# A hybrid decoder layer: first weight piece in two halves with a PSUM bank per column block, first norm by token half, 17 products of ones ahead of the first transposes

## What is computed

```
h = x
h = h + ssd_mixer(rms_norm(h, mixer_norm), w_in, conv_w, ..., w_out)
h = h + cross_attention(rms_norm(h, xattn_norm), rms_norm(mem, mem_norm), xa_w_q, xa_w_kv, xa_w_o)
h = h + moe_ffn(rms_norm(h, ffn_norm), w_router, w_gate_up (32 x 1024 x 2048), w_down (32 x 1024 x 1024))
out = rms_norm(h, final_norm)

ssd_mixer:  proj = h @ w_in                      # 1024 x 5152: z 2048, xbc 3072, dt 32
            xbc  = silu(causal_conv4(xbc) + conv_b)
            dt   = softplus(proj_dt + dt_bias)   # then a chunked scan over 2 chunks of 128 tokens
```

## Time and profile before

| | |
|---|---|
| median of 3 runs | 1261.46 us (1261.38 to 1263.63) |
| the profiled execution's own time | 1264.04 us |
| its span | 1262.2 us |
| mean granted PE clock | 0.994 of 2.4 GHz |
| PE busy | 1173.2 us (93%) |
| DVE, ACT busy | 390.8 us, 265.4 us |
| DMA | 454.28 MB, mean 360 GB/s |

### The profile page before, as it was taken

How to read it: one execution, slowest core, us unless ns; L and a number is a source line. 1 busy time by engine, 2 the same in 40 slices (tenths; PEclk the granted TensorE clock), 3 DMA queues, 4 the chain that set the end, 5 groups by cost and what they waited for, 6 DMA issues and landing times.

```text
span 1262.2 us, 15351 instructions
## 1 busy us (share of the span) xinstructions
PE 1173.2 (93%) x6172; PEld 617.9 (49%) x6172; DVE 390.8 (31%) x705; ACT 265.4 (21%) x409; POOL 7.5 (1%) x27
## 2 busy tenths in 40 slices
PE   7999999999999999999889899999999998999996
PEld 6998887888733433333333333334433333333432
DVE  5887676645411211111111111212111111122112
ACT  6555444445210101010100001101101011011102
POOL 1000000000000000000000000000000000000000
PEclk9999999999999999999999999989999999999999
DMA  9454323478799999999999999999999999999996
GB/s 323 166 200 135 133 71 131 152 309 302 286 414 427 428 429 428 429 428 429 427 428 430 428 429 427 429 427 428 427 429 429 427 428 429 387 427 430 426 426 255
DMA packets 55654, 454.28 MB, mean 360 GB/s; under 512 B 6396, under 2 KB 6564, under 8 KB 30532
## 3 DMA queue, kind: packets, MB, share of 16 engines
q1 hardware_dynamic: 55440, 453.74, 87.0%
q10 hardware_dynamic: 180, 0.07, 0.0%
HBM read 452.74 MB, written 1.05 MB: 360 GB/s over the span
## 4 chain that ended last, share of the span: by engine, by line
PE 52%; DMA 42%; DVE 3%; SPq 1%; issue 1%; ACT 1%; DVEq 1%; ACTq 0%
DMA ring<-in_moe_w_down 41%; PE ps L882 13%; PE ps L906 11%; PE ps L559 3%; PE ps L561 3%; PE ps L560 3%; PE ps L916 2%; PE ps L858 2%; PE ps L574 2%; PE ps L576 2%; PE ps L575 2%; PE ps L693 1%; DMA wring<-in_ssd_w_in 1%; DVE wlo L1397 1%; PE ps L893 1%; SPq L430 1%
## 5 line engine op out<-in xcount | busy, mean ns | idle before, releaser
L906 PE MATMUL ps<-ring,wring 128*64 128x512 f32 x960 | 216.8, 597 | 54.7 <-DMA ring<-in_moe_w_down 54.7
L882 PE MATMUL ps<-ring,wring 128*64 128x512 f32 x1024 | 223.3, 594 | 0.0
L906 PEld LDWEIGHTS ps<-ring,wring 128*64 128x64 f32 x960 | 64.9, 137 | 194.8 <-issue 110.8
L1026 ACT ACTIVATE wring<-ps 128x512 f32<-128x512 f32 (+2 forms) x101 | 52.4, 534 | 501.6 <-PE ps L882 431.0
L1725 DVE COPY wring<-ps 128x512 f32<-128x512 f32 x32 | 22.1, 691 | 405.1 <-PE ps L882 405.1
L882 PEld LDWEIGHTS ps<-ring,wring 128*64 128x64 f32 x1024 | 72.1, 137 | 139.7 <-issue 139.6
L1733 DVE TENSOR_TENSOR wring<-ps,bguT 128x512 f32<-128x512 f32 x64 | 41.2, 686 | 302.6 <-PE ps L893 302.6
L882 PE MATMUL ps<-mid,wring 128*64 128x512 f32 x512 | 114.6, 600 | 1.0 <-DVE wring L1733 1.0
L1026 ACT ACTIVATE ysb<-ps 128x512 f32<-128x512 f32 x36 | 21.5, 598 | 272.1 <-PE ps L906 252.3
L882 PEld LDWEIGHTS ps<-mid,wring 128*64 128x64 f32 x512 | 35.8, 138 | 68.6 <-issue 68.3
L858 PEld LDWEIGHTS ps<-wring 128*128 128x128 f32 x480 | 55.8, 192 | 23.5 <-issue 23.5
(11 more groups left out here) (316 smaller groups left out, 1407.1 us busy)
## 6 DMA issues: line engine op xcount, KB each, us to landing
ring<-in_moe_w_gate_up SPq DMA_DIRECT2D x64, 2048.0 KB, 23.1
ring<-in_moe_w_down SPq DMA_DIRECT2D x60, 2048.0 KB, 25.5
mid<-in_moe_w_gate_up SPq DMA_DIRECT2D x32, 2048.0 KB, 23.4
wring<-in_moe_w_gate_up SPq DMA_DIRECT2D x16, 2048.0 KB, 26.4
hs<-in_moe_w_gate_up SPq DMA_DIRECT2D x16, 2048.0 KB, 27.9
wring<-in_ssd_w_in SPq DMA_DIRECT2D x10, 2048.0 KB, 8.2
wring<-in_xa_w_kv SPq DMA_DIRECT2D x4, 2048.0 KB, 8.2
wring<-in_ssd_w_out SPq DMA_DIRECT2D x4, 2048.0 KB, 7.8
```

Source lines behind the costliest of these rows:

```text
L882: last = mm(ps[a][SLOTS * half:SLOTS * (half + 1), :], xs[:, m, c % 2, :], w[:, kk, c0:c0 + 512], start=s + kk == 0, stop=s + kk == GP)
L906: last = mm(ps[D_BANK][SLOTS * half:SLOTS * (half + 1), :], act[:, k, :], w[:, kk, 512 * half:512 * (half + 1)], start=k == 0, stop=k == K ...
L1026: return nc.scalar.activation(out_, in_, func, **kw)
```

## The change

1. x's two token halves get a semaphore each (`ld_x[t]`), and ACT starts on half 0 when it has landed; ACT waits for the first POOL step alone instead of all constants.
2. Piece 0 is loaded by two transfers, row blocks 0 to 3 (`w_first`) and 4 to 7 (`w_ready[0]`). `first_projection` replaces `project_T`: all four column blocks with row blocks 0 to 3, then all four with 4 to 7, each block summed in a bank of its own (0, 1, 6, 7). `u_ps` is raised after blocks 0 and 1, and after 2 and 3, of the second pass.
3. PE makes 17 products `ones` x `ones` (128 x 128 float32) into bank 0 as soon as `ones` is there; nothing reads them.
4. The transposes of the parameter rows go behind the transposes of token half 0. On DVE the copy to `parT` goes behind both halves of the norm, and the constants `iota0`, `sel`, ... behind the copies of `xT`.
5. DVE copies row blocks 0, 1, 4, 5 of `xT`, ACT 2, 3, 6, 7. dt's products use bank 4 instead of 6. Convolutions of piece 0 read the new banks.

The diff, cut to its core:

```diff
+        def u_out(p, b, m):
+
+            return ps[(0, 1, 6, 7)[2 * b + m]][:, 0:SEQ] if p == 0 else ps[2 * (p % 2) + b][:, SEQ * m:SEQ * (m + 1)]
...
-                sp.dma_start(h[:, t, :], x[P * t:P * (t + 1), :]).then_inc(ld_x, 16)
+                sp.dma_start(h[:, t, :], x[P * t:P * (t + 1), :]).then_inc(ld_x[t], 16)
             for r0, v in ((16, mem_norm), (24, ssd_norm), (40, ffn_norm)):
                 n = v.shape[0] // P
                 sp.dma_start(rows_b[r0:r0 + n, :], v.rearrange("(c p) -> c p", p=P)).then_inc(ld_rows, 16)
-            sp.dma_start(wpiece(0), pieces[0]).then_inc(w_ready[0], 16)
+            sp.dma_start(wpiece(0)[:, 0:4, :], pieces[0][:, 0:4, :]).then_inc(w_first, 16)
+            sp.dma_start(wpiece(0)[:, 4:8, :], pieces[0][:, 4:8, :]).then_inc(w_ready[0], 16)
...
-            pe.wait_ge(cst_done, 1)
-            pe.wait_ge(ld_rows, 112)
-            tr(ps[7][:, 0:120], rows_a[0:120, :], ident[0:120, 0:120])
-            tr(ps[7][:, 128:176], rows_b[0:48, :], ident[0:48, 0:48]).then_inc(par_ps, 1)
+            pe.wait_ge(cst_step, 1)
+            for _ in range(WARM):
+                mm(ps[0][:, 0:P], ones, ones, start=True, stop=True)
+            pe.wait_ge(cst_step, 2)
+
+            def parameters(t):
+                pe.wait_ge(ld_rows, 112)
+                tr(ps[7][:, 0:120], rows_a[0:120, :], ident[0:120, 0:120])
+                tr(ps[7][:, 128:176], rows_b[0:48, :], ident[0:48, 0:48]).then_inc(par_ps, 1)
...
-            norm_transposes(0, xn0, 2)
+            norm_transposes(0, xn0, 2, parameters)
...
-                        last = mm(ps[6][HEADS * j:HEADS * (j + 1), 0:SEQ], wdt[:, 4 * half + j, :],
+                        last = mm(ps[4][HEADS * j:HEADS * (j + 1), 0:SEQ], wdt[:, 4 * half + j, :],
...
-            def project_T(n, banks, src, done, guard):
-
-                w = take(n)
-                for b in range(2):
-                    guard(b)
-                    for m in range(2):
-                        for n_, k in enumerate((0, 4, 1, 5, 2, 6, 3, 7)):
-                            if b == m == 0:
-                                pe.wait_ge((nt_dve, nt_act)[k // 4], k % 4 + 1)
-                            c0 = (2 * b + m) * P
-                            last = mm(ps[banks[b]][:, SEQ * m:SEQ * (m + 1)], w[:, k, c0:c0 + P], src[:, k, :],
-                                      start=n_ == 0, stop=n_ == KD - 1)
-                    last.then_inc(done, 1)
+            def first_projection():
+
+                w = wpiece(0)
+                pe.wait_ge(par_sb, 1)
+                for half in range(2):
+                    pe.wait_ge(*((w_ready[0], 16) if half else (w_first, 16)))
+                    for b in range(2):
+                        for m in range(2):
+                            for k in range(4 * half, 4 * half + 4):
+                                if b == m == 0:
+                                    pe.wait_ge((nt_dve, nt_act)[k // 2 % 2], 2 * half + k % 2 + 1)
+                                c0 = (2 * b + m) * P
+                                last = mm(u_out(0, b, m), w[:, k, c0:c0 + P], xT[:, k, :],
+                                          start=k == 0, stop=k == KD - 1)
+                        if half:
+                            last.then_inc(u_ps, 1)
...
-            project_T(W_U, (0, 1), xT, u_ps, lambda b: None)
+            first_projection()
...
+                    if n == 0:
+                        act_.wait_ge(ld_x[t], 16)
...
-            def norm_out(n, dst, gains, bank0=0):
...
+            def first_rows():
+
+                for k in (2, 3, 6, 7):
+                    act_.wait_ge(nt_ps, k // 2 + 1)
+                    fn(xT[:, k, :], ps[2 + k // 2][:, SEQ * (k % 2):SEQ * (k % 2 + 1)], ACT.Copy,
+                       scale=parT[:, g_mix + k:g_mix + k + 1]).then_inc(nt_act, 1)
...
-            act_.wait_ge(cst_done, 1)
+            act_.wait_ge(cst_step, 1)
             load_sqrt()
-            act_.wait_ge(ld_x, 32)
             norm_stats(0, h, xn0)
             act_.wait_ge(par_sb, 1)
-            norm_out(0, xT, g_mix, 2)
+            first_rows()
...
+                    last = fn(cv[:, n % 4, m, :], u_out(p, b, m), ACT.Identity,
...
-            dve.wait_ge(cst_done, 1)
-            v.tensor_scalar(iota0[:, :], iota[:, 0:NE], -1.0, None, ALU.add)
-            dve.drain()
-            v.tensor_scalar(sel[:, :], iota0[:, :], col[:, 1:2], None, ALU.is_equal)
-            dve.drain()
-            v.memset(acx[64:128, :, :], 1.0)
-            v.memset(nacx[0:64, :, :], 1.0)
-            v.tensor_reduce(ingrp[:, :], sel[:, :].rearrange("p (g j) -> p g j", g=GROUPS), AX_X, ALU.add)
-            v.tensor_reduce(by8[:, :], sel[:, :].rearrange("p (g j) -> p j g", g=GROUPS), AX_X, ALU.add)
-            dve.wait_ge(par_ps, 1)
-            v.tensor_copy(parT[:, 0:120], ps[7][:, 0:120])
-            v.tensor_copy(parT[:, 120:168], ps[7][:, 128:176]).then_inc(par_sb, 1)
...
-            def norm_out(n, dst, gains, bank0=0):
...
+            def first_rows():
+
+                for k in (0, 1, 4, 5):
+                    dve.wait_ge(nt_ps, k // 2 + 1)
+                    v.tensor_scalar(xT[:, k, :], ps[2 + k // 2][:, SEQ * (k % 2):SEQ * (k % 2 + 1)],
+                                    parT[:, g_mix + k:g_mix + k + 1], None, ALU.mult).then_inc(nt_dve, 1)
...
-            for t in range(TC):
-                norm_chunk(0, t, xn0, h)
-            norm_out(0, xT, g_mix, 2)
+            norm_chunk(0, 0, xn0, h)
+            norm_chunk(0, 1, xn0, h)
+            dve.wait_ge(par_ps, 1)
+            v.tensor_copy(parT[:, 0:120], ps[7][:, 0:120])
+            v.tensor_copy(parT[:, 120:168], ps[7][:, 128:176]).then_inc(par_sb, 1)
+            dve.drain()
+            first_rows()
+            dve.wait_ge(cst_done, 1)
...
             dve.wait_ge(xz_hi, 1)
             v.tensor_tensor(xz[1], xT[:, :, :], xz[0].bitcast(F32), ALU.subtract)
             w_lo(1, 0)
...
+                        src = u_out(p, b, m)[:, 0:SEQ - back]
...
-            v.tensor_copy(dtT, ps[6][:, 0:SEQ]).then_inc(dtT_sb, 1)
+            v.tensor_copy(dtT, ps[4][:, 0:SEQ]).then_inc(dtT_sb, 1)
```

More of the change, by code:

```diff
@@ L59 @@
 HSLOTS = 4
+WARM = 17
 def build(nc, x, mem, mixer_norm, xattn_norm, mem_norm, ffn_norm, w_in, conv_w, conv_b, dt_bias, a_log,
@@ L211, in build @@
         sums = ps_all[:, 4 * 512:8 * 512].rearrange("p (t n c) -> p t n c", n=2, t=TC)
-        (ld_x, ld_mem, ld_rows, ld_small, ld_bg, ld_g, ld_bdn, ld_wdt, ld_wrt, cst_step, cst_done) = (
-            sem(n) for n in ("ld_x", "ld_mem", "ld_rows", "ld_small", "ld_bg", "ld_g", "ld_bdn", "ld_wdt",
+        ld_x = [sem(f"ld_x{t}") for t in range(TC)]
+        (ld_mem, ld_rows, ld_small, ld_bg, ld_g, ld_bdn, ld_wdt, ld_wrt, cst_step, cst_done) = (
+            sem(n) for n in ("ld_mem", "ld_rows", "ld_small", "ld_bg", "ld_g", "ld_bdn", "ld_wdt",
                              "ld_wrt", "cst_step", "cst_done"))
+        w_first = sem("w_first")
         w_ready = [sem(f"w_ready{s}") for s in range(3)]
@@ L532, in dt_tokens @@
                 for t in range(TC):
-                    last = mm(ps[6][:, SEQ + HEADS * t:SEQ + HEADS * (t + 1)], dtT[:, P * t:P * (t + 1)], sel[:, :],
+                    last = mm(ps[4][:, SEQ + HEADS * t:SEQ + HEADS * (t + 1)], dtT[:, P * t:P * (t + 1)], sel[:, :],
                               start=True, stop=True)
                 last.then_inc(dt_ps, 1)
-            def project_T(n, banks, src, done, guard):
-                w = take(n)
-                for b in range(2):
-                    guard(b)
-                    for m in range(2):
-                        for n_, k in enumerate((0, 4, 1, 5, 2, 6, 3, 7)):
-                            if b == m == 0:
-                                pe.wait_ge((nt_dve, nt_act)[k // 4], k % 4 + 1)
-                            c0 = (2 * b + m) * P
-                            last = mm(ps[banks[b]][:, SEQ * m:SEQ * (m + 1)], w[:, k, c0:c0 + P], src[:, k, :],
-                                      start=n_ == 0, stop=n_ == KD - 1)
-                    last.then_inc(done, 1)
+            def first_projection():
[13 more added lines that the diff above has]
+                            last.then_inc(u_ps, 1)
             def split_tokens(n, t, bank, x_hl, k0=0, ks=range(KD), start=True, stop=True):
@@ L1083, in tap @@
                     w = convw_c + 3 * NCONV + c0 + m
-                    last = fn(cv[:, n % 4, m, :], ps[2 * (p % 2) + b][:, SEQ * m:SEQ * (m + 1)], ACT.Identity,
+                    last = fn(cv[:, n % 4, m, :], u_out(p, b, m), ACT.Identity,
                               scale=parT[:, w:w + 1], bias=parT[:, convb_c + c0 + m:convb_c + c0 + m + 1])
@@ L1397, in w_lo @@
                 v.tensor_tensor(lo_, raw_, hi.bitcast(F32), ALU.subtract).then_inc(wl_ok, 1)
-            for t in range(TC):
-                norm_chunk(0, t, xn0, h)
-            norm_out(0, xT, g_mix, 2)
+            norm_chunk(0, 0, xn0, h)
```

(13 more changed lines are left out.)

## The result

Over 22 runs of each kernel, the changed one took 1264.88 us (median; 1263.09 to 1267.33) and the one before 1263.55 us (1261.38 to 1265.13). The ratio is 1.0014, with a 95% interval of 1.0008 to 1.0019: 1.0 to 2.4 us slower, within the 0.2% that the chances call "same". The two medians differ by 1.33 us, where +1.2 us was forecast; the time itself, 1264.88, lies above the stated range, which ended at 1263.9.

A forecast was written before the change was run, and what follows sets the result against it. DVE, fed by piece 1's landing, was taken to set the start of `dt_tokens`, and PE the pace after it. Nothing gained plus 1.2 us of slow clock on 1261.46 gave 1262.7 us, range 1260.8 to 1263.9.

The forecast's parts named there:

- the first term of the sum: The base for the whole kernel: median of earlier runs, 1261.46 us, to which 1.2 us were added.
- What bounds the kernel: Up to 36 us: piece 1's landing, ACT's rounding, then DVE until `dt_tokens` at 34.73; PE sets the pace afterwards.
- Start of the projection: First projection on PE: half 0 of x 1.1 us sooner, first transpose about 8.2, projection starting about 10.3.
- The 17 products: PE's start: they end between 5.2 and 9.0 and buy fast transposes, about 1 to 1.8 us off the path.
- Projection, banks, order: First projection keeps 14.05 us, ending about 24.3; `tap(0)` isn't delayed, and moved banks and constants cost nothing.
- even with a start at 12.7: First `u_ps` at 23.2 plus 1.00 for `tap(0)` would still come before `conv(0)` at 24.59.
- Transfers: SP's queue: piece 1 lands at 18.13 again despite one more issue; 0 us taken, bounds 0 and 4.7.
- The wait: PE before `dt_tokens` waits 2.9 us for DVE's copy (between 0.5 and 3.7), instead of 0.5.
- The clock: Behind PE's wait before `dt_tokens` the clock falls to half, costing 1.2 us of a full 1.45.
- The allowance for slow time inside the wait: At PE's wait before `dt_tokens`: 1.2 us taken instead of 1.45, since part of the slow stretch may lie there.
- says the same of such gaps: Claim that the Trainium skill, too, has a gap between bursts of products bring back TensorE's half-rate clock.
- the level and the scatter: Whole kernel: a base of 1261.46 us, with 0.7 us (range's low end) and 0.6 us (high end) of scatter.

The follow-up runs named there:

- e1: The changed kernel with 12 unread products of ones filling PE's wait before `dt_tokens`; ratio 0.9996 to the kernel before.
- e2: The changed kernel with `dt_tokens` moved behind the second pair of column blocks of piece 1; ratio 0.9984 to the kernel before.
- e6: The changed kernel with piece 0 loaded by one transfer again, both passes of the projection waiting for it; ratio 1.0009 to the kernel before.
- e8: The changed kernel with `dt_tokens` behind the second pair, DVE's second low half of piece 3 before `conv(3)`, and the 264 us wait filled; ratio 0.9977.
- e10: The changed kernel with `dt_tokens` behind the second pair, the 264 us wait filled, and piece 3 split earlier on ACT and DVE; ratio 0.9967, 1259.19 us.
- e5: The kernel before with only the 17 products of ones added ahead of the parameter transposes; ratio 0.9998 to the kernel before.
- e3: The changed kernel without the 17 products of ones at the start; ratio 0.9997 to the kernel before.
- e4: The kernel before with only `dt_tokens` moved behind the second pair of column blocks of piece 1; ratio 1.0012 to the kernel before.
- e11: The changed kernel with 5 unread products of ones in PE's wait before `dt_tokens`; ratio 0.9997 to the kernel before.
- e7: The kernel before with 9 products of ones in PE's wait at 264 us, ahead of the query products; ratio 0.9995.

## Why the prediction was right, and where it was wrong

The mechanism held: nothing gained on the path, a longer wait of PE, and the clock behind it. The step that failed is the first term of the sum, the level of 1261.46 us to which the 1.2 us were added; the runs put it at 1263.55.

**What bounds the kernel: right.** `dt_tokens` waits for DVE, DVE for piece 1; e1 and e2 show it from both sides.

**Start of the projection: right.** 9.98 against 10.3, with the first transpose at 7.46 against 8.2. ACT began on x 1.3 us sooner (4.77 against 6.09) and not 1.1; the rest is that the estimate left the two parameter copies before the first norm on DVE's way, which the change had moved. First half landed 6.2 us after its issue, at 9.0, against 9.5.

**The 17 products: right.** 5.41 us, between the bounds of 3.8 and 7.6, over before the transposes.

**Projection, banks, order: right.** 14.05 us again, end 23.96 against 24.3; `tap(0)` not delayed. That it would be covered "even with a start at 12.7" was reckoned at the fast clock alone; e6, with a start at 12.10 and a slow stretch behind it, kept DVE waiting 1.06 us. The constants that moved behind the norm cost nothing: DVE still stood idle 4.30 us before the first low half of piece 1.

**Transfers: right.** Piece 1 landed at 17.75, not later. The 0.4 us that it came sooner lies within the scatter: the kernels with the one transfer of before had ACT start on it between 17.69 and 18.16 in five profiles, those with the two halves between 17.68 and 17.78 in eight. A small help from the halves isn't excluded.

**The wait: right.** 2.88 us against 2.9.

**The clock: right in kind, a little too cheap.** I took 1.2 us from a full 1.45; the profile shows 1.51 and the ratio 1.0 to 2.4 us. The allowance for slow time inside the wait wasn't needed: the slow spacing began about 0.7 us after PE had resumed at 34.34. That the change in time came out so near is in part luck: in this profile the mark is 1.12 us late, the 1.51 less the 0.39 by which piece 1 happened to land sooner, and the sum took one fall in every run more than before, which no row then showed.
The Trainium skill's account ("TensorE: Matmul & The Clock Gate", Part 1, HAM oscillation) of a gap that brings the slow clock back is what the trace shows at 35 us. The gap of the page's example is longer than this wait of 2.88 us, so the prediction's "says the same of such gaps" claimed more than the page gives: that a wait of this length can be followed by a fall is what these runs show.

**Where it failed: the level and the scatter.** The sum was put on 1261.46, the median of three runs, and the range allowed 0.7 us of scatter. 22 runs gave 1263.55, and 89 runs beside the experiments spread from 1261.2 to 1265.6. Two of the three had fallen near the lower end; that was bad luck, but the spread was there to be seen: the third was 1263.63, and the text itself stated that the profiled execution took 1264.04, a quarter of the evidence then at hand, and took the level from the median all the same. It was an ordinary run. The 0.7 us is the distance of the profiled span, 1262.2, from that median; but a span is some 1.8 us shorter than its own execution's time (1264.04 here), so it compares unlike things. With a base of 1263.55 the sum gives 1264.75, 0.13 from the measured time, and the term that was mis-sized is the base, by 2.1 us.

**What the scatter is made of** is open in the main. In 89 runs of the kernel before, time and lost clock go together (correlation 0.65, 0.40 us for each us lost). Kernels with fewer waits scatter less: standard deviation 1.16 us before, 0.72 in e2, 0.68 in e8, 0.32 in e10 (six runs); but e5, which keeps the waits, has 0.80. And e10 has lost as much clock as others (9.3 us), in its profile mostly behind 815 us, and is the fastest all the same. A fall that costs only where PE is the pace would explain it; that wasn't tested, nor which falls make up the 4 us.

## What to carry to other kernels

An engine's earlier finish is worth only what the next thing that it waits for lets through; follow the chain from the landing of the data, and ask of every wait on it which other queue it holds up. In this kernel a longer wait of TensorE was not free even though nothing in it was late: the products behind it may run at half the clock (0.214 us apart instead of 0.12 for 3.3 us), and filler products in the wait, or a reordering that removes it, give that back. Take the level of a forecast from every execution at hand, the profiled one too, and the width of the range from their spread.

## What was not expected of the hardware

- Whether the clock falls behind a wait of about the same length differs from profile to profile. Behind the wait of 2.3 to 2.8 us near 264 us the granted clock fell to 0.5 in some profiles (before, e1, e2, e5, e6) and stayed at 1.00 in others (changed: 1.00 from 262 to 268.6; e3, e4, e11). A wait of 1.5 us in e3 and of 1.8 us in e11 was followed by a fall, one of 1.65 us in e4 at 55 us was not. In the four profiles with that wait filled (e7 to e10) the clock stayed at 1.00 there.
- Products of a constant with itself, which nobody reads, kept the clock up: behind 12 of them, 2.84 us, it was 1.00 from 34 to 40 us in e1.
- The landing of the same 2 MB transfer varies by some 0.4 us between executions of the same transfers.
